# Splitting finished mixer tiles for the output projection during the last two gate chunks, in the first block and the mLSTM block

## The reference, cut to what matters

```python
# first block: 4 differential-attention heads, 4 retention heads, each 128 wide
mixed = jnp.concatenate([oa * jax.nn.silu(ga), orr * jax.nn.silu(gr)], axis=-1)
x = x + jnp.einsum('bse,ed->bsd', mixed, w_out[l])
...
# second block, layer 0: 4 mLSTM heads, each 256 wide, both directions summed and normalised
hs = hs * lax.rsqrt(jnp.mean(hs * hs, axis=-1, keepdims=True) + EPS)
return (hs * o_gate).astype(h.dtype) @ w_out
...
# then a gated MLP; layer 1: windowed attention and another gated MLP; a last RMS norm
```

## Time and profile before

| | us |
|---|---|
| median of 3 runs (lowest to highest) | 1482.77 (1482.47 to 1485.17) |
| the profiled execution's own time | 1483.84 |
| its span, first to last instruction | 1482.1 |
| TensorE busy in the span | 1461.5 (99%) |
| VectorE busy | 788.6 (53%) |
| ScalarE busy | 585.0 (39%) |
| GpSimd busy | 56.2 (4%) |
| mean granted clock of TensorE | 0.996 of full speed |

### The profile page before, as it was taken

How to read it: one execution, slowest core, us unless ns; L and a number is a source line. 1 busy time by engine, 2 the same in 40 slices (tenths; PEclk the granted TensorE clock), 3 DMA queues, 4 the chain that set the end, 5 groups by cost and what they waited for, 6 DMA issues and landing times.

```text
span 1482.1 us, 18429 instructions
## 1 busy us (share of the span) xinstructions
PE 1461.5 (99%) x7286; PEld 1194.5 (81%) x7286; DVE 788.6 (53%) x1530; ACT 585.0 (39%) x1097; POOL 56.2 (4%) x108
## 2 busy tenths in 40 slices
PE   8999999999999899999999999999999999999998
PEld 8878776889888688888888887866688888888887
DVE  5666653656656764443344445677664443344443
ACT  5654541444443443231223233567653231223222
POOL 0011000000000000000000000111100000000000
PEclk9999999999999999999999999999999999999999
DMA  6112020132112122322322224110022312322221
GB/s 239 63 58 85 30 85 29 43 118 82 57 58 85 57 86 86 114 68 99 121 97 85 89 79 139 58 57 30 29 86 86 114 68 100 130 87 86 89 88 66
DMA packets 22038, 123.20 MB, mean 83 GB/s; under 512 B 2368, under 2 KB 4544, under 8 KB 10816
## 3 DMA queue, kind: packets, MB, share of 16 engines
q1 hardware_dynamic: 21952, 122.02, 24.1%
HBM read 119.91 MB, written 2.10 MB: 82 GB/s over the span
## 4 chain that ended last, share of the span: by engine, by line
PE 94%; DVE 3%; ACT 1%; DMA 1%; issue 0%; SPq 0%; POOL 0%; DVEq 0%; ACTq 0%
PE PS L261 85%; PE PS L284 5%; PE PS L293 3%; DVE WL L229 1%; DMA RAW<-in_w_in 1%; DVE FT L238 0%; PE PS L256 0%; ACT FT L216 0%; DVE ACC L229 0%; ACT WH L216 0%; DMA FT<-in_pos 0%; ACT FR L216 0%; DVE G L229 0%; SPq L310 0%; DVE FP L238 0%
## 5 line engine op out<-in xcount | busy, mean ns | idle before, releaser
L261 PE MATMUL PS<-XH,WH 128*128 128x512 f32 x1080 | 431.7, 400 | 0.0
L261 PE MATMUL PS<-XH,WL 128*128 128x512 f32 x1080 | 420.9, 390 | 0.0
L261 PE MATMUL PS<-XL,WH 128*128 128x512 f32 x1080 | 420.7, 390 | 0.0
L261 PE MATMUL PS<-FR,WH 128*128 128x512 f32 (+1 forms) x1132 | 340.5, 383 | 4.9 <-DVE WL L229 2.0
L229 DVE TENSOR_TENSOR WL<-RAW,WH 128x512 fp32r<-128x512 f32 (+3 forms) x334 | 273.1, 859 | 113.8 <-ACT WH L216 112.1
L216 ACT ACTIVATE WH<-RAW 128x512 fp32r<-128x512 f32 (+3 forms) x334 | 236.4, 758 | 154.2 <-PE PS L261 148.7
L261 PEld LDWEIGHTS PS<-FR,WH 128*128 128x128 f32 x1132 | 207.9, 188 | 47.9 <-ACT WH L216 2.9
L261 PEld LDWEIGHTS PS<-XH,WH 128*128 128x128 f32 x1080 | 202.8, 188 | 48.3 <-issue 7.7
L261 PEld LDWEIGHTS PS<-XH,WL 128*128 128x128 f32 x1080 | 202.7, 188 | 43.0
L261 PEld LDWEIGHTS PS<-XL,WH 128*128 128x128 f32 x1080 | 203.0, 188 | 42.6 <-issue 3.1
L261 PE MATMUL PS<-FR,WL 128*128 128x512 f32 (+1 forms) x566 | 215.7, 381 | 0.0
(11 more groups left out here) (118 smaller groups left out, 1283.7 us busy)
## 6 DMA issues: line engine op xcount, KB each, us to landing
RAW<-in_f_in SPq DMA_DIRECT2D x44, 1024.0 KB, 4.8
RAW<-in_w_in SPq DMA_DIRECT2D x13, 1024.0 KB, 4.8
RAW<-in_m_in SPq DMA_DIRECT2D x12, 1024.0 KB, 4.8
RAW<-in_f_oa SPq DMA_DIRECT2D x16, 768.0 KB, 4.4
RAW<-in_f_ob SPq DMA_DIRECT2D x16, 640.0 KB, 3.9
RAW<-in_a_in SPq DMA_DIRECT2D x6, 1024.0 KB, 4.8
RAW<-in_w_out SPq DMA_DIRECT2D x4, 1024.0 KB, 4.7
RAW<-in_m_out SPq DMA_DIRECT2D x4, 1024.0 KB, 4.9
```

The costliest lines, as they stand in the source:

```text
L261: f = lambda e: e.matmul(o, l, r, start=start, stop=stop, skip_group_check=True)
```

## The change

`out_proj` is no longer a generator itself. Called when the streams are put together, it defines its parts, stores a function `early` in `st["out"]`, and returns the generator `run_out`, whose body is the old one. When a projection reaches gate chunk 2, it copies that function to `st["early"]`; from there on a call of `feed` that finds no weight part to issue calls `early` instead. `early` splits at most one mixture tile: the next in order, if it is ready and due by TensorE's clock, and if two FR buffers are free beyond the reserve. `run_out` takes `early` away again when it starts. The attention block's output projection stores its function as well, but nothing there enables it. `parts` is renamed `both`.

```diff
     def feed():
         if parts:
             w_part()
+        elif "early" in st:
+            st["early"]()
...
             elif c[0] == "g":
+                if n == 2:
+                    st["early"] = st["out"]
                 j, h, l, wt = w_use()
...
         mt = {}
 
-        def parts(k):
+        def both(k):
             (a, fa), (b, fb) = fr.take(), fr.take()
             tk = split(G[:, k, :], FR[:, a, :], FR[:, b, :], ready["mix", k], fa, fb)
             mt[k] = (a, b, tk)
...
             if ok:
-                parts(k)
+                both(k)
             return ok
 
+        def early():
+            k = len(mt)
+            if k < KT and ("mix", k) in ready and due(ready["mix", k]) <= PE.t and len(fr.q) >= 2 + st.get("fr_kept", 0):
+                both(k)
+
+        def run_out():
+            st.pop("early", None)
+            full = []
...
+        st["out"] = early
+        return run_out()
...
             if c[0] == "g":
+                if hd == 2:
+                    st["early"] = st["out"]
                 j, h, l, wt = w_use()
```

More of the change, by code:

```diff
@@ L993, in make @@
             if ok:
-                parts(k)
+                both(k)
             return ok
[L997 to L1045, removed]
-                    adds()
[L1047 to L1052, removed]
@@ L1053, in out_proj, with piece, adds @@
-        for k in range(KT):
-            ready.pop(("mix", k))
-            ready.pop(("mixl", k), None)
+        def early():
[5 more added lines that the diff above has]
+            full = []
+            def piece(c, cur, k, u):
+                j, h, l, wt, bs, todo = cur
+                b, fb = bs[u]
+                ma, mb, tk = mt[k]
+                t = mm3(PS[:, b, :], (h[:, k, u * 128:u * 128 + 128], l[:, k, u * 128:u * 128 + 128]),
+                        (FR[:, ma, :], FR[:, mb, :]), k == 0, k == KT - 1, wt[k], tk, fb)
+                if k == KT - 1:
+                    full.append((2 * c + u, b, t))
+                return t
+            def adds():
+                while full:
+                    add_tile(*full.pop(0), next_w)
+            two = []
+            for c in range(2):
+                x = w_use(c == 0)
+                two.append([*x, [bank.take(), bank.take()], deque((k, u) for k in range(KT) for u in range(2))])
+            while two[0][5] or two[1][5]:
+                c = next((c for c in range(2) if two[c][5] and two[c][5][0][0] in mt), None)
+                if c is None:
+                    if ("mix", len(mt)) in ready:
+                        yield [ready["mix", len(mt)]]
+                    if not make():
+                        yield None
+                    continue
+                k, u = two[c][5].popleft()
+                yield [two[c][3][k], mt[k][2], two[c][4][u][1]]
+                while len(mt) < KT and ("mix", len(mt)) in ready and due(ready["mix", len(mt)]) <= PE.t:
+                    if not make():
+                        break
+                t = piece(c, two[c], k, u)
+                feed()
+                if not two[c][5]:
+                    w_done[two[c][0]] = t
+                    if c == 0:
+                        w_prep(two[0][0] + 2)
+                    adds()
+            assert w_split[two[0][0] + 2] is not None
+            for c in (2, 3):
+                x = w_use()
+                cur = [*x, [bank.take(), bank.take()], None]
+                for u in range(2):
+                    for k in range(KT):
+                        yield [cur[3][k], cur[4][u][1]]
+                        t = piece(c, cur, k, u)
+                        adds()
+                        if k % 2:
+                            feed()
+                w_done[cur[0]] = t
+            for a, b, tk in mt.values():
+                fr.put(a, t)
+                fr.put(b, t)
+            for k in range(KT):
+                ready.pop(("mix", k))
+                ready.pop(("mixl", k), None)
```

## The result

| | before | after |
|---|---|---|
| median, us (lowest to highest) | 1484.14 (1482.47 to 1485.17), 6 runs | 1475.38 (1472.43 to 1479.68), 6 runs |
| profiled execution, us | 1483.84 | 1473.93 |
| its span, us | 1482.1 | 1472.1 |
| mean granted clock in it | 0.996 | 0.998 |

The ratio is 0.9946, with a 95% interval of 0.9927 to 0.9965: 8.0 us faster (5.2 to 10.8); the two medians differ by 8.8. A second set, run beside the last experiments, gave 0.9947 (0.9934 to 0.9961). The forecast was 6.47 us.

The account below looks back on a forecast made before the run. TensorE was taken as the bound, busy 1461.5 of 1482.1 us, with dummies and low clock hiding waits. 4.02 (first block) + 2.45 (mLSTM) = 6.47 us off 1482.77 gave 1476.3 us; range 1473.4 to 1480.2.

Parts of the forecast that it names:

- First block: After g3, the stretch with 30 dummy matmuls before the output projection's first piece goes: 4.02 us, at least 3.5.
- tile 7's remainder: First block: lands at 269.65 today, TensorE needs it at 269.74, so it is in time and adds no wait.
- cover: ScalarE and VectorE have free time under full TensorE in g2 and g3; splits cost nothing, uncovered 7.5 us.
- the parts that stand ahead of the tiles: First block, ScalarE: second output chunk's four parts, held back by TensorE from 258.97, stand before the first mixture tile at 261.06.
- mLSTM: After g3, pieces fill waits of 2.44 and 1.10 us and end the low clock: 2.45 us taken, bounds 0 to 5.01.
- The chain's shift: mLSTM, VectorE: four of six tile splits leave head 3's normalisation chain, so tiles 6 and 7 come 2.45 us sooner.
- A: Rival: in the mLSTM a wait moves to head 3's transposes or tiles 4 to 6, clock falls: 1477.8 us, chance 0.14.
- B: Rival: only the first block gains, head 3's chain in the mLSTM keeps its end: 1478.8 us, chance 0.13.
- C: Rival: second-chunk pieces fill all mLSTM waits, 4.02 + 5.01 = 9.03 us won: 1473.7 us, chance 0.12.
- D: Rival: `early` finds tiles not due, or the plan loses elsewhere what it won: 1482.8 us, chance 0.08.
- E: Rival: in g2's second tile a split's copy waits for an unread FR buffer, delaying the head: 1485.9 us, chance 0.07.
- The sum: First block plus mLSTM, 4.02 + 2.45 = 6.47 us won, median 1476.3 us; 5 to 8 us won had chance 0.46.

Follow-up runs that it names:

- order-only run: Kernel before with no early splits; `run_out` splits all finished tiles ahead of the second chunk's parts in all three mixers: 1479.11 us, ratio 0.9973.
- one-chunk run: Changed kernel, but in the mLSTM's output projection no second-chunk piece goes before the first chunk is through: 1479.65 us, ratio 0.9984.
- mLSTM-only: Changed kernel with early splits enabled only in the mLSTM block, the first block left as before: 1480.19 us, ratio 0.9973.
- one-tile kernel: Changed kernel, but `early` may split only tile 0, in both blocks: 1480.36 us, ratio 0.9981.
- start-filled kernel before: Kernel before, without the change, plus ten dummy matmuls ahead of the first norm's one-column matmuls: 1482.50 us, ratio 0.9992.
- everything and fill: Changed kernel plus start dummies, pieces chosen by due splits, third chunk's parts earlier, finished tiles split first, and eight dummies at the first MLP's weight wait: 1470.75 us.
- the two kernels with everything: Changed kernel plus start dummies, due-based piece choice, earlier third-chunk parts and finished tiles first: 1472.09 us; with eight first-MLP dummies more, 1470.75 us.
- start-filled kernel: Changed kernel plus ten dummy matmuls ahead of the first norm's one-column matmuls: 1473.24 us, ratio 0.9935.

## Why the prediction was right, and where it was short

*First block.* Right in place and size: 4.05 to 4.14 us in eight profiles, forecast 4.02. Seven tiles were split early, four and three, as counted; tile 7's remainder was no new wait. Its cover held. One thing was put too simply: the parts that stand ahead of the tiles were named as the cause, and the order-only run shows that to be under half of it (1.82 us); most of the rest is VectorE's gate multiplication, behind which the remainders would still stand.

*mLSTM.* The mechanism was right and the term too small: 2.45 forecast, 3.64 to 3.66 measured. Four splits in g2 and none in g3 came as forecast. The chain's shift was 1.95 us (tiles 6 and 7 split at 25.89 against 27.83 us after g3's end), not 2.45. The missing half microsecond stands at one place of head 3's chain, where VectorE now waits for TensorE's last value products: from the addition before it to the last normalisation it is 0.79 us (504.73 to 505.52), and was 0.34 (513.47 to 513.81). VectorE, changed kernel, then kernel before:

```profile
505.52 0.16 DVE L234 TENSOR_SCALAR SC<-PS 128x1 f32<-128x1 f32 x1 [0.37 <-PE PS L284]
```

```profile
513.81 0.16 DVE L234 TENSOR_SCALAR SC<-PS 128x1 f32<-128x1 f32 x1
```

What the forecast named as possible, but put at nothing in its sum, is that TensorE in the shorter stretch also gets more done. Counted from behind: of 64 pieces at 0.68 us, the kernel before had 47 left at tile 6's first piece, since the MLP begins 32.06 us later (rows of the kernel before, TensorE):

```profile
521.09 0.71 PE L261 MATMUL PS<-FR,WH 128*128 128x512 f32 x2
...
553.15 0.39 PE L261 MATMUL PS<-XH,WH 128*128 128x512 f32 x1
```

The changed kernel has 543.17 - 512.77 = 30.40 us there, less the 0.93 that the late third chunk costs (521.28 less the end of the piece before it, 520.35): 43. Four second-chunk pieces more, 2.72 us, were done in the waits. 1.95 + 2.72 - 0.93 = 3.74, against 3.64. These counts are of the profiles; the one-chunk run agrees, as far as it goes. It holds back all nine second-chunk pieces, not only the four, and loses 4.6 us, more than the mLSTM's whole gain.

*The rivals.* A's wait is there, at the transposes of head 3 and at tile 4, as described, and the clock did fall behind it in the profiles of the mLSTM-only and one-chunk kernels, to 0.57 and 0.65; in the changed kernel's it didn't. It differs from one execution to the next, and belongs in the range rather than beside it. B is out: the mLSTM alone gives 4.0 us. C's mechanism, second-chunk pieces in the waits, was at work too, but not in full: four pieces and new waits, 3.64 us and not 5.01. D is out. E is out: no FR<-G copy waits for TensorE in the rows above.

*The sum.* 4.02 + 2.45 forecast; 4.05 + 3.64 measured, 1.2 us more, all of it in the second term. 1476.3 was forecast and 1475.38 measured, inside 1473.4 to 1480.2. That the time came out within 1 us is partly luck: the forecast started from the 1482.77 of three runs, and six runs of the same kernel have 1484.14; the base was 1.4 us too low and the gain, by the ratio, 1.5 us too small, and the two nearly cancel.

## What to carry to other kernels

On an engine that works in order, what counts is not when an operand is ready but behind which waiting instruction its preparation is written: small conversions belong ahead of the last long product, at points where that engine's list holds nothing that waits. When a chain on another engine sets a stretch, price the change by two terms, the chain's shift and the independent work that the main engine can do meanwhile. And look at what the freed engine runs into next: three new waits, 2.85 us in all, came up behind the filled ones, and reordering against them gave back 1.06 there (0.33 of it was lost again in attention).

## What the runs showed of the hardware

The same short pause is followed by a low clock in one execution and not in another. At 20 us TensorE waits for ACC and then runs eight one-column matmuls. Wait and clock, changed kernel and one-tile kernel, whose instructions there are the same:

```profile
20.72 1.05 PE L261 MATMUL PS<-ONE,ACC 128*128 128x1 f32 x8 [1.20 <-DVE ACC L229]
```

```profile
22.00:24.00 2.00, 2.00 (x12) 0.55 0.00 0
24.00:26.00 2.00, 2.00 (x13) 0.60 0.99 287
```

```profile
20.64 1.05 PE L261 MATMUL PS<-ONE,ACC 128*128 128x1 f32 x8 [1.22 <-DVE ACC L229]
```

```profile
22.00:24.00 2.00, 2.00 (x19) 1.00 0.00 0
24.00:26.00 2.00, 2.00 (x19) 1.00 1.01 287
```

So too in the first MLP, where TensorE waits for weights: behind a wait of 2.10 us the clock of the start-filled kernel before was 0.57 from 900 to 904 us (1.71 us lost, by the table); behind the same 2.10 us the changed kernel kept 1.00. With dummies at that wait, in the kernel with everything and fill, it was 1.00 in the one profile.

The unfilled waits of the kept profiles can be counted. Behind the start's wait (1.20 to 2.27 us) the clock fell in six profiles of ten, behind the mLSTM's wait of 2.44 to 2.47 in five of five (in four of them with the 1.10 us after it), behind the new one of 1.43 to 1.45 in two of five, behind the first MLP's (1.9 to 2.5) in three of thirteen. A fall cost 1.5 us in the mLSTM and 1.5 to 1.8 in the first MLP, by the table. The Trainium skill, "TensorE: Matmul & The Clock Gate", Part 1, says that the gate's view of the activity runs on its own and isn't aligned with the kernel. That fits these counts; no run here shows the gate's view itself.

So an unfilled wait of this kind carries a chance of a fall, and the runs' scatter fits that: 7 and 3 us in the changed kernel's two sets, some 2 us or less in the two kernels with everything and in the one with the start filled, over few runs each. What a fill costs depends on its length. In the first MLP it was shorter than the wait and cost next to nothing (+0.22 us by the table, and -0.10 to +0.48 in the unfilled profiles whose clock stayed up); at the start it was longer than the wait, by 0.4 us in the start-filled kernel and 0.7 to 0.8 in the two with everything, and that was paid back out of what it saved. What it writes must be free, or it waits as well, as in the mLSTM.
